# Narrow products for two decay levels of an HGRN2 mixer, with one product fewer per attention score and rearranged stage boundaries

## What is computed

```
# HGRN2: S_t = diag(exp g_t) S_{t-1} + k_t v_t^T ; o_t = S_t^T q_t      (16 heads, 128 x 128)
decay = exp(where(t >= s, b_t - b_s, -inf))          # b = cumulative sum of g, per channel d
A = einsum('bhtd,bhsd,bhtsd->bhts', q, k, decay)
# forgetting attention
logit[t, s] = q_t . k_s / sqrt(d) + F[t] - F[s]      # s <= t, F = cumsum(log_sigmoid(fz))
# indexer of the hybrid layer
iscore = sum_h relu(q_idx[h] . k_idx / 8) * w[h]     # 16 heads of 64; the best 64 keys are kept
```

## Time and profile before

| | us |
|---|---|
| median of 3 runs | 3307.46 (3303.35 to 3310.0) |
| the profiled execution | 3306.82, its span 3305.1 |
| PE (TensorE) busy | 3249.8 (98% of the span) |
| PEld (weight loads) busy | 3074.8 (93%) |
| DVE (VectorE) busy | 2317.5 (70%) |
| ACT (ScalarE) busy | 1641.2 (50%) |
| 16 DMA engines | 48.9%, 172 GB/s |
| mean granted clock of TensorE | 0.994 of full |

### The profile page before, as it was taken

How to read it: one execution, slowest core, us unless ns; L and a number is a source line. 1 busy time by engine, 2 the same in 40 slices (tenths; PEclk the granted TensorE clock), 3 DMA queues, 4 the chain that set the end, 5 groups by cost and what they waited for, 6 DMA issues and landing times.

```text
span 3305.1 us, 62706 instructions
## 1 busy us (share of the span) xinstructions
PE 3249.8 (98%) x25192; PEld 3074.8 (93%) x25192; DVE 2317.5 (70%) x3772; ACT 1641.2 (50%) x2198; POOL 7.8 (0%) x27
## 2 busy tenths in 40 slices
PE   8999999999999999999999999999999999999998
PEld 7999999899999989999999999998899889987787
DVE  7767667554455656555568998985699558999855
ACT  5444444667674545555544444444444444444444
POOL 0000000000000000000000000000000000000000
PEclk9999999999999999999999999999999999999999
DMA  4444445444444445454454455555555555555554
GB/s 180 151 155 152 152 157 179 141 155 158 153 164 166 170 140 185 156 184 169 168 185 168 173 192 180 188 180 191 191 183 187 182 196 183 183 177 183 181 207 153
DMA packets 99062, 569.94 MB, mean 172 GB/s; under 512 B 9424, under 2 KB 30288, under 8 KB 31568
## 3 DMA queue, kind: packets, MB, share of 16 engines
q1 hardware_dynamic: 98896, 567.58, 48.9%
HBM read 565.45 MB, written 2.10 MB: 172 GB/s over the span
## 4 chain that ended last, share of the span: by engine, by line
PE 85%; DVE 10%; ACT 2%; DVEq 1%; DMA 1%; issue 1%; ACTq 0%; SPq 0%
PE bank L504 20%; PE bank L505 20%; PE bank L506 20%; PE bank L997 5%; PE bank L999 5%; PE bank L998 5%; DVE wl L1474 4%; PE bank L664 2%; DVE hot_a L2048 1%; PE bank L606 1%; PE bank L851 1%; PE bank L856 1%; PE bank L923 1%; DVE gates_b L2055 1%; ACT wh L1028 1%
## 5 line engine op out<-in xcount | busy, mean ns | idle before, releaser
L504 PE MATMUL bank<-hh,wh 128*128 128x256 f32 x5696 | 1613.7, 283 | 14.2 <-DVE hl L1507 9.1
L505 PE MATMUL bank<-hl,wh 128*128 128x256 f32 x5696 | 1582.5, 278 | 0.0
L506 PE MATMUL bank<-hh,wl 128*128 128x256 f32 x5696 | 1581.9, 278 | 0.0
L1474 DVE TENSOR_TENSOR wl<-raw,wh 128x1024 fp32r<-128x1024 f32 x1052 | 1253.1, 1220 | 418.5 <-ACT wh L1028 410.4
L1028 ACT ACTIVATE wh<-raw 128x1024 fp32r<-128x1024 f32 x1052 | 1051.9, 1050 | 341.6 <-DMA raw<-w_in_a 133.9
L504 PEld LDWEIGHTS bank<-hh,wh 128*128 128x128 f32 x5696 | 1074.8, 189 | 26.6 <-issue 14.4
L505 PEld LDWEIGHTS bank<-hl,wh 128*128 128x128 f32 x5696 | 1075.7, 189 | 8.1 <-issue 7.5
L506 PEld LDWEIGHTS bank<-hh,wl 128*128 128x128 f32 x5696 | 1075.9, 189 | 0.0
L997 PE MATMUL bank<-wh,ah 128*128 128x512 f32 x1024 | 402.3, 393 | 6.4 <-DVE al L2098 6.3
L999 PE MATMUL bank<-wl,ah 128*128 128x512 f32 x1024 | 398.9, 390 | 0.0
L998 PE MATMUL bank<-wh,al 128*128 128x512 f32 x1024 | 398.6, 389 | 0.0
(11 more groups left out here) (351 smaller groups left out, 2773.8 us busy)
## 6 DMA issues: line engine op xcount, KB each, us to landing
raw<-peer_u SPq DMA_DIRECT2D x128, 1024.0 KB, 4.9
raw<-peer_v SPq DMA_DIRECT2D x128, 1024.0 KB, 4.9
raw<-w_in_c SPq DMA_DIRECT2D x64, 1024.0 KB, 4.9
raw<-w_in_a SPq DMA_DIRECT2D x63, 1024.0 KB, 4.9
raw<-w_kv SPq DMA_DIRECT2D x32, 1024.0 KB, 4.9
raw<-w_in_b SPq DMA_DIRECT2D x32, 1024.0 KB, 4.9
raw<-w_out_a SPq DMA_DIRECT2D x16, 1024.0 KB, 4.9
raw<-w_out_b SPq DMA_DIRECT2D x16, 1024.0 KB, 4.9
```

What stands on the lines that cost most here:

```text
L504: eng.matmul(out, h_[:, k, :], high[:, k, :], start=(k == 0), stop=False)
L505: eng.matmul(out, h_[:, k, :], low[:, k, :], start=False, stop=False)
L506: last = eng.matmul(out, low_rows(c, k), high[:, k, :], start=False, stop=(k == KC - 1))
L1474: eng.tensor_tensor(low_half_out(c, half), raw_half(c, half), high_half(c, half).bitcast(F32), ALU.subtract).then_inc(lo_ready, 1)
```

## The change

What it does, part by part:

1. Stage A, levels 5 and 6 (h = 32 and 64). Instead of four matmuls with 128 keys as weights and 64 queries, level 5 does eight with 32 keys by 32 queries, level 6 four with 64 keys by 64 queries. Each writes to the partitions of its keys. VectorE copies them with two and one plain COPY, all four head tiles at once, without masks.
2. Stage F, scores. The gate weights are laid twice into the FG unit, at columns 0 to 15 and 32 to 47, so that F[t] and -F[s] come out on different partitions. `fqry` holds F in rows 0 to 15 and ones in the rest, `fkey` the negated F in rows 32 to 47 and ones in the rest, `selF` is `fkey` times a selector of the head's two rows. One matmul then adds both terms: L728's goes, L727's takes `fqry` in place of `ones`, and `selO` and its copies go.
3. Stage F, start. The high and low parts of units 3 and 4 and the squares of the keys move ahead of the parts of the gate chain; the two MEMSET move to before the norm.
4. Stage X. `index_scores` uses banks 4 to 7, waits for the `relu` of four heads before, the queries of odd groups go to bank 2 in place of bank 0 (and the wait for `ckv_read` goes), and the last group's scores are issued between the halves of C's first product; the wait for the last `relu` moves behind C's third product.
5. Outputs. `outputs_high` waits for half a product less for the first four chunk pairs, and in stage C the first four pairs are split inside the last pair, ahead of its tail.
6. U to V. In the last turn of `gate_turns` the last `gate` and `act_low` come first, then the low parts, then the selection rows; ScalarE's `keep_low_gates` of that turn comes one `high_part` earlier. From V2 to V3 `act_low` comes ahead of `add_experts`.

```diff
@@ a_levels (TensorE)
                     for n in range(2 * NT):
-                        last = eng.matmul(bank[:, at + n * (P // 2):at + (n + 1) * (P // 2)], KL[l][:, n * P:(n + 1) * P],
-                                          halves(QL[l][:, n * P:(n + 1) * P], h)[:, :, 1, :], start=True, stop=True)
+                        if l < NARROW:
+                            eng.matmul(bank[:, at + n * (P // 2):at + (n + 1) * (P // 2)], KL[l][:, n * P:(n + 1) * P],
+                                       halves(QL[l][:, n * P:(n + 1) * P], h)[:, :, 1, :], start=True, stop=True)
+                        else:
+                            for a in range(0, P, 2 * h):
+                                eng.matmul(bank[a:a + h, at + n * (P // 2) + a // 2:at + n * (P // 2) + a // 2 + h],
+                                           KL[l][:, n * P + a:n * P + a + h], QL[l][:, n * P + a + h:n * P + a + 2 * h], start=True, stop=True)
@@ a_masks (VectorE)
+                    if l >= NARROW:
+                        level = bank[:, at:at + T].rearrange("p (n t) -> p n t", n=2 * NT)
+                        for a in range(0, P, 2 * h):
+                            eng.tensor_copy(AT[a:a + h, :, a + h:a + 2 * h], level[a:a + h, :, a // 2:a // 2 + h])
+                        continue
@@ f_scores (TensorE)
-                        eng.matmul(o, ones[:, :], selF[:, j, 0:n], start=False, stop=False)
-                        last = eng.matmul(o, fcum[:, tt], selO[:, j, 0:n], start=False, stop=True)
+                        last = eng.matmul(o, fqry[:, tt], selF[:, j, 0:n], start=False, stop=True)
@@ index_scores (TensorE)
-                    b = 6 + n % 2
-                    if past_zero(n - 1):
-                        eng.wait_ge(s["relu_ready"], n - 1)
+                    if past_zero(n - 3):
+                        eng.wait_ge(sX["relu_ready"], n - 3)
...
-            index_scores(3)
-            eng.wait_ge(s["relu_ready"], IDX_HEADS)
@@ c_body (TensorE)
-                project("C", 0, i, hh, hl)
+                product(i, BASE["C"], B[0][:, 0:T], hh, hl, None, (lambda: index_scores(3)) if first else None)
+                one_product("C", 0, 1, i, hh, hl)
@@ stage F, start (ScalarE)
-            stream_norm("F", [kh, hh])
+            stream_norm("F", [kh, hh], first_keys)          # ksq behind the fourth chunk pair of hh
+            high_part(0, BASE["F"] + 3)
+            high_part(0, BASE["F"] + 4)
             eng.wait_ge(s["z_ready"], 1)
@@ stage F, start (VectorE)
+            low_part(0, BASE["F"] + 3)
             eng.wait_ge(bias_in, 16)
...
                                      op1=ALU.add).then_inc(s["z_ready"], 1)
+            low_part(0, BASE["F"] + 4)
             eng.wait_ge(s["l_ready"], 1)
@@ outputs_high (ScalarE)
-                eng.wait_ge(mm_done, 2 * (BASE[name] + units))
                 for c in range(first, first + count):
+                    eng.wait_ge(mm_done, 2 * (BASE[name] + units) - (1 if 2 * c < FH else 0))
@@ c_body (ScalarE; the same on VectorE with outputs_low)
+                if final:
+                    outputs_high("C", 0, PAIRS // 2)
@@ gate_turns (VectorE), last turn of the last eight
-                        low_half(last_turn, u, 1)
-                        gate(b, last_turn, c, (b + 1, 0, c + 2 - PER_PAIR), False)
+                        gate(b, last_turn, c)
+                        act_low(b, 0, 0)
+                        low_half(last_turn, u, 0)
+                        low_half(last_turn, u, 1)
+                        hot_rows(b + 1, 0, 1)
+                        eng.drain()
+                        gate_rows(b + 1, 0, 1)
@@ v_turns (VectorE)
-                act_low(b, 0, 0)
...
+                    if gating and n == BJ - 1:
+                        act_low(b + 1, 0, 0)
                     if n % (BJ // 2) == BJ // 2 - 1:
                         add_experts(b, n // (BJ // 2))
```

More of the change, by code:

```diff
@@ L235, in program @@
         probT_f = sb_in(m, "probT_f", [P, 2, SC])
[L236 removed]
+        both = sb_in(m, "both", [P, HEADS])
+        fz = [(prob_f if n < 3 else probT_f)[0:FG_ROWS, :, :].rearrange("p a b -> p (a b)")[:, (n % 3) * T:(n % 3 + 1) * T]
               for n in range(5)]
@@ L494, in _, with product @@
         def _(eng):
-            def product(i, c, out, high, low, fresh=None):
+            def product(i, c, out, high, low, fresh=None, between=None):
                 h_ = wh[c % RAW]
@@ L507, in product @@
                     last.then_inc(mm_done, 1)
+                    if half == 0 and between is not None:
+                        between()
             def project(stage, s, i, high, low, fresh=None):
@@ L839, in c_body @@
                 eng.wait_ge(s["xc_ready"], i + 1)
+                if first:
+                    eng.wait_ge(sX["relu_ready"], IDX_HEADS)
                 if past_zero(i):
@@ L1218, in f_body @@
                 u = BASE["F"]
-                high_part(i, u + 3)
                 if not first:
+                    high_part(i, u + 3)
                     f_square_out(i - 1)
[L1222 to L1225, removed]
+                    f_square_keys(i)
+                    high_part(i, u + 4)
                     f_rstd_out(i - 1)
@@ L1308, in _, with c_body @@
             s = sC
-            def c_body(i, first):
+            def c_body(i, first, final=False):
                 u = BASE["C"]
@@ L1406, in gelus @@
                     last_turn = isinstance(i, int) and i > 0
-                    if b >= 1:
+                    if b >= 1 and not (last_turn and c == PER_PAIR - 1):
                         keep_low_gates(b - 1, i, c)
@@ L1778, in f_body @@
                 u = BASE["F"]
-                low_part(i, u + 3)
+                if not first:
+                    low_part(i, u + 3)
                 for j in range(2):
-                    eng.tensor_scalar(selF[:, j, :], fneg[:, :], ident[:, ds(i * 2 + j, 1)], None, ALU.mult)
-                    last = eng.tensor_copy(selO[:, j, :], ident[:, ds(i * 2 + j, 1)].broadcast_to([P, T]))
+                    last = eng.tensor_scalar(selF[:, j, :], fkey[:, :], both[:, ds(i * 2 + j, 1)], None, ALU.mult)
                 last.then_inc(s["sel_ready"], 1)
-                low_part(i, u + 4)
                 if not first:
+                    low_part(i, u + 4)
                     gated_out(s, i - 1, 5, ors_f, on_f, gate_f, "b_onorm", "F")
@@ L1829, in _ @@
             eng.wait_ge(s["crs_ready"], 1)
-            for n, c in enumerate((0, 2, 1, 3)):
+            for c in range(RC):
                 last = eng.scalar_tensor_tensor(out=ckvT[:, c, :], in0=latent_bank(c),
                                                 scalar=col("ckv", c), in1=crs[:, :], op0=ALU.mult, op1=ALU.mult)
-                if n == 1:
-                    last.then_inc(s["ckv_read"], 1)
             last.then_inc(s["ckv_ready"], 1)
@@ L2056, in gate_rows, with gate @@
                                   gT[:, tt, :].unsqueeze(3).broadcast_to(k), ALU.mult).then_inc(s["pairs_ready"], 1)
-            def gate(b, i, c, after=None, rows_first=True):
+            def gate(b, i, c, after=None):
                 n = i * PER_PAIR + (b * BJ + c)
@@ L2064, in gate @@
                                          op0=ALU.mult, op1=ALU.add)
-                if after is not None and rows_first:
+                if after is not None:
                     hot_rows(*after)
```

86 lines of the change are left out of this document (48 added, 38 removed).

## The result

The changed kernel takes 3264.9 us (median, 3263.7 to 3268.0) where the kernel before takes 3308.7 in the same set: a ratio of 0.987, 95% interval 0.985 to 0.989. The same kernel in a later set took 3267.5 against 3307.4 (0.988, 0.986 to 0.990). The forecast was 3267.0. Its profiled execution took 3268.0, its span 3266.3 us, 38.8 less than before.

What follows compares the result with a forecast made beforehand. TensorE, busy 98% of the span, was taken as the bound, so only its own work or stalls could shrink; the six parts sum to -39.8 us, 3306.8 - 39.8 = 3267.0 us, with 8 in 10 held by 3254 to 3285.

Steps and rivals of the forecast that it cites:

- the sum: Whole kernel: -2.2 - 10.5 - 7.5 - 12.2 - 2.4 - 5.0 = -39.8 us for the six parts.
- The load of 32 columns: Stage A, level 5: a weight load takes time in proportion to its width, 0.028 us for each of 16 records.
- The load of 64 columns: Stage A, level 6: a weight load takes time in proportion to its width, 0.056 us for each of 8 records.
- the change of shape: Stage A, TensorE: each change of the array's shape costs 0.2 us, three in a pair, 0.6 us.
- rival 3: Whole kernel, best case: narrow records at 0.030 us without switching cost, nothing given back, 3257 us; chance 0.11.
- The 0.4 us left for ScalarE's roots: Start of F: 0.4 us allowed for ScalarE's two head-norm roots, which come just about when TensorE asks.
- the give-back: C's first pair: small weights delay the fifth unit's load and the chain to the transposes; 2.0 us given back.
- a fall in a new place: Whole kernel, sign against the forecast: it is wrong if the granted clock falls in a new place; no size given.
- the give-back foretold: Middle of V2: TensorE starts 1.6 us sooner, meets VectorE's adds that much later and gives about 1.3 us back.
- Rival 5: Products' two paces may be picked anew; all of A, F and C slower: some +30 us at most, 3297 us; chance 0.04.

Runs made afterwards that it cites:

- the altered order: The changed kernel with level 5's records issued first all of one column block, then all of the other; 3266.8 us in a single execution.
- the interleaved run: The changed kernel with the records of levels 5 and 6 interleaved, nine changes of the array's shape in a pair instead of three; 3274.5 us.
- part 1 alone: The kernel before with only the change's part 1 (narrow records for levels 5 and 6); 3306.7 us against 3307.8, ratio 0.9998.

## Why the prediction was right, and where it was not

Each of the six parts gained where and by what the prediction said, and the total came out near the forecast: the changed kernel's trace is 38.8 us shorter, the two medians 43.8 and 40.0, the sum was 39.8. What failed are two prices in part 1, and a loss of clock that was not counted in part 4. The sizes, with the products' pace taken out where it can be:

| part | predicted | measured in the traces |
|---|---|---|
| 1, two levels | -2.2 | -5.3 (-5.7 in the blocks, +0.4 in the records behind) |
| 2, F's scores | -10.5 | -11.1 |
| 3, F's start | -7.5 | -8.4 (F's 19.5 less part 2) |
| 4, indexer | -14.2, +2.0 back | X -13.3; C -2.4 +1.6, and +0.9 +1.7 back: -11.5 |
| 5, C to OC | -2.4 | -2.35, the stall is gone |
| 6, U to V | -5.0 | -5.8 |
| pace | 0 | +6.2 |

In part 4 the C terms are: the first half product, 5.2 us at the lower clock before and 2.7 now; the last group of scores, moved there, 1.6 us; the longer wait for `prob_c`; the half product behind it. That last 1.7 us is of the changed kernel's first execution alone. Parts 1, 2 and 4 were also run by themselves or undone; parts 3, 5 and 6 have no run of their own, and their sizes are read from the rows and starts of the two traces.

**Part 1** was mis-sized. Two of its terms failed. The load of 32 columns was put at 28 ns in proportion to its width; one block's records do stand 32 ns apart, but two blocks work side by side, and 16 records took 0.25 us in place of 0.45 (that the blocks, not a lower price of the record, did this is what the altered order showed). The load of 64 columns was right (58 ns against 56). And the change of shape was put at 0.2 us, from the indexer's row; it costs 0.09 in the changed kernel's own block (0.98 less 0.25 and 0.46, over three) and 0.13 in the interleaved run. Only rival 3 had room for this, for another reason. The rule that the prediction cites from the Trainium skill, that going to another mode drains the engine, agrees with these runs in that a change costs time; that it is a drain no row shows. The rule right beneath it, that tiles run in parallel, was the one that mattered, and the prediction left it out.

Yet the time hardly shows these 5.3 us: part 1 alone gave 1.2 us in the median (at most 3.6 by the interval), and undoing it cost 1.6 to 4.2. One thing fits: in the two traces with full levels A's products stand 1.1 us in sum beyond the faster pace, in the eleven with narrow ones 1.4 to 4.1. The rows show where. The 96 product records right behind the levels take one of two times, 10.99 us (as from 191.81 to 202.79 before) or 11.39 (as from 189.64 to 201.03 after). With full levels the two take turns from pair to pair in both traces. With narrow ones they take turns in three traces and are nearly always the longer in the others, in all seven pairs of the changed kernel's first trace. So in most traces the narrow block leaves the products behind it at the slower pace more often; why, and why not in all, stays open, and with one trace of most kernels so does whether it explains the medians.

**Parts 2 and 3** held, and the third matmul put back split F's gain as the sum had it. The 0.4 us left for ScalarE's roots was not needed beyond small gaps.

**Part 4** held in its mechanism down to the give-back: the small weights held up the fifth unit's load, ScalarE waited 11.3 us for it, and the transposes waited longer. The wait grew by 0.9 us where 2.0 was expected, but the clock fell behind it, in a new place, which cost 1.7 more; the prediction had named a fall in a new place as a sign that it is wrong, and in this term it was. It is not a fixed cost. In the nine traces that have part 4 and the old load order the wait was 1.9 to 2.7 us, and the clock fell behind it in five of them. The prediction had read in the earlier trace rows that idleness is followed by half clock, and did not apply it to the wait that it foresaw itself.

**Part 6**: the middle of V2 waits 1.3 us, which is the give-back foretold; the starts of V0, V1, V2 and V3 gained 1.9, 1.9, 1.6 and 0.4 us, the last of them the 1.6 of its own wait less the 1.2 by which the wait in V2 grew. Each wait for `al` was worth a little more than its row, since the distance of starts also holds what the row of the wait leaves out.

**Rival 5**, the pace, was right in naming the two paces. It left open what picks them: two executions of one program differ in them, and whether the order of work has a share, as A and OF suggest, isn't shown. The pace cost this trace some 6.2 us, and it hid what the sum had too small: 3.1 us in part 1 and about 2 in parts 2, 3 and 6. So the total's agreement is in part luck.

## What to carry to other kernels

Small products that each fill only a part of the array pay by their place: put consecutive ones on different column blocks, and gather them, since each change of shape costs about as much as one full record. When a stall is removed, list which transfers and chains start from its end, and price each wait that you expect to remain with and without the clock's loss behind it. Compare kernels by stage: stages whose code is the same and that moved even so are the measure of what the trace can't attribute.

## What the runs showed of the hardware

- Float32 records on one block of 32 columns stand 32 ns apart, on two blocks in turn 16, on four (with 16 moving columns) 8; with 64 columns 58, and half of that on the two halves in turn. Full records stand 111 ns apart. A change of shape costs 0.09 to 0.13 us.
- The split products' records run at 113.5 or 118 ns, at full granted clock, and one program can have either in the same stage: 179 or 172 records in 20 us of U0 in two executions of the same kernel.
- A burst of some 170 short records in 1.5 us, on the first pass through a loop's code, was followed by 4.1 to 4.3 us in which TensorE issued nothing, in both kernels that have the burst; later passes showed none.
- Waits of 2.3 to 2.7 us on TensorE in C's first pair were followed by a stretch at the lower clock level in five traces (2.3, 2.3, 2.3, 2.7, 2.7 us) and not in three (2.5, 2.7, 2.7), the changed kernel's two executions (2.3 and 2.5) being one of each kind. Behind a wait of 1.9 and those of 1.4 us there the clock stayed full.
